# A threshold for one short weight block, the place of two sigmoid gates among weight splits, and the turn of six transposes in a two-layer fp32 kernel

## The chip, the cores and the metric

The kernel runs on one core of one Trainium2 chip. The metric is the device time of one execution in microseconds (us); lower is better.

## The reference

Two transformer layers over 1024 tokens of 1024 channels, batch 1, all in fp32. The first layer is attention of two kinds (eight grouped heads over all tokens, eight heads over a neighbourhood of the 16 x 64 grid). The second has a recurrence (RWKV7) and a latent attention, whose outputs are merged by gates. Cut to what the change touches:

```python
def mla_branch(c_q, c_kv, k_pe, z, positions, g_q, w_uq, g_kv, w_ukv, w_out_b):
    q = (rmsnorm(c_q, g_q) @ w_uq).reshape(bsz, seq, B_HEADS, QK_NOPE_DIM + QK_ROPE_DIM)
    kv = (rmsnorm(c_kv, g_kv) @ w_ukv).reshape(bsz, seq, B_HEADS, QK_NOPE_DIM + V_HEAD_DIM)
    ...

def second_block(...):
    u = rmsnorm(h, g_pre)
    proj = u @ w_in
    feat_a, z_a, c_q, c_kv, k_pe, z_b, gate_logits = split_cols(proj, ...)
    y_a = rwkv7_branch(feat_a, z_a, ...)
    y_b = mla_branch(c_q, c_kv, k_pe, z_b, ...)
    gates = jax.nn.sigmoid(gate_logits + b_gate)
    g_a, g_b = gates[..., :D_MODEL], gates[..., D_MODEL:]
    merged = g_a * y_a + g_b * y_b
    h = h + rmsnorm(merged @ w_o, g_post)
```

`c_q` (256 columns) and `c_kv` (128 columns) are the "compressed columns" below.

## The kernel before

Five programs, one per engine, are written out by hand (`pe_program`, `act_program`, `dve_program`, `pool_program`, `sp_program`); each waits on semaphores that others raise. There is no scheduler: the order on an engine is the order in which its program issues.

**Products.** Every fp32 matrix product is three matmuls of rounded parts: high by high, high by low, low by high. One such step of 128 rows of the inner dimension is called a product here (L992, L993, L994 in the dense part of the second layer; L695 to L697 in the merges).

**Weights.** The weights come as 52 blocks (`wplan`), each of up to 2048 elements per partition. SyncE fetches block n into one staging tile `WST` (`fetch`, L3103), ScalarE rounds it into a high part in pieces of 512 columns (`part`, L1416), GpSimd subtracts to get the low part (L2809). A fetch waits for the splits of the block before it, since there is one staging tile; a split waits for the end of the block that used the same one of two buffers. TensorE waits on entering a block for its last piece. The class `Weights` is run by every engine's program in step and says when the pieces of the next block are issued; `tick` is called with the products done so far in the block:

```python
while self.coming is not None and self.coming[0] <= self.b + (...) and \
      self.ticks[0] >= (20 if self.b in EARLY else 36) + 9 * self.ticks[1]:
    self.ticks[1] += 1
    self.split(False)
    if self.b in EARLY:
        self.fetch_next()
```

So the four pieces of the successor come after 36, 45, 54 and 63 products, and in blocks that are in `EARLY` after 20, 29, 38 and 47, with the next fetch issued as soon as the staging tile is free. `leave` issues what is left at the end of the block. Most blocks count 96. `OUT1` is 13, so `OUT1 + 5` is block 18: the last 160 columns ahead of the paired blocks, which counts 8 tiles x 8 steps x 3 x 160/512 = 60.

**The second layer's input product** (`dense_walk`) goes through blocks 17 to 37. The first ones (17, 18, half of 19) run alone. After that, `Interleave` mixes the dense products with the recurrence: 16 `unit`s in two flows; after every round of unit steps `fill` issues as many dense products as fit beside them. At the end, a third generator, `late`, is advanced once per turn, each turn with a fill of 2.2 us of dense products: it squares the compressed columns (L1806), sums them (L2589), raises the mean to the power -1/2 on GpSimd (L2815), scales the columns (L2603, L2604 on VectorE), transposes them (L1218 on TensorE, six groups of four), and splits them into high and low (L1813 on ScalarE, L2609 on VectorE). Each engine's `late` counts turns, so that the steps stand at the right place of its program. What is left of the dense products comes in `rest`.

**Merges.** Eight blocks of 256 output columns (`MERGES`), four groups of 12 matmuls each. Per 128 columns a gate is loaded by SyncE into one of two tiles `GA` (L3390) and goes through a sigmoid on ScalarE (`output_gate`, L1942); VectorE multiplies (L2753, L2758), adds the branches (L2760), and ScalarE and VectorE split the sum for the output product (L1962, L2735). `ahead`, at a block's start, issues the whole split of the next block. TensorE takes the eight PSUM banks in turn for the groups.

Of the kernel before, what the change touches and what calls it, by code (L numbers as in the profile page):

```python
# [148 lines left out]
def build(nc, a, out):  # L149
    ctx = ExitStack()  # L150
    with ctx:
# [194 lines left out]
        wplan = []  # L346
# [89 lines left out]
        half_p, w_lo, power_p, rope_p, zero_p, prep_p, lat_p, band_lo = by(  # L436
            POOL, "half_p", "w_lo", "power_p", "rope_p", "zero_p", "prep_p", "lat_p", "band_lo")

        EARLY = (0, 1, 2, 3, OUT1 - 1, OUT1, OUT1 + 1, UQ - 2, UQ - 1, *range(UQ + 2 + len(MERGES), len(wplan) - 1))

        class Weights:

# [220 lines left out]
        def pe_program(e, w):  # L663
# [544 lines left out]
                yield NORM_US  # L1208

            def late():  # L1210
                for _ in range(LANDED + 8):
                    yield
                for g in range(2):
                    for k in range(3):
                        ps = bank_at(("ct", k, g), k, (lat_a, ("ct", k, g)), (lat_v, ("ct", k, g)))
                        w.wait_ge(*lat_v["cn", 4 * g + 3])
                        for i in range(4):
                            m = e.transpose(ps[:, tile128(i)], CN[:, 4 * g + i, tile128(k)], ident)  # L1218
                        m.then_inc(lat_tr.sem, lat_tr.up(("ct", k, g)))
                        yield  # L1220
# [179 lines left out]
        def act_program(e, w):  # L1400
# [399 lines left out]
            def late():  # L1800
                for _ in range(LANDED):
                    yield
                for x in range(4):
                    w.wait_ge(*d_cn[x // 2]["all"])
                    two = slice(2 * x, 2 * x + 2)
                    e.activation(SQC[:, two, :], CN[:, two, 0:384], ACT.Square).then_inc(lat_a.sem, lat_a.up(("sq", x)))  # L1806
                    yield
                for _ in range(4):
                    yield
                for g in range(2):  # L1810
                    for k in range(3):
                        w.wait_ge(*lat_tr["ct", k, g])
                        e.activation(CTH[:, k, half512(g)], psum(("ct", k, g)), ACT.Identity, scale=vec("g_q", k) if k < 2 else vec("g_kv")).then_inc(  # L1813
                            lat_a.sem, lat_a.up(("ct", k, g)))
                        yield
# [129 lines left out]
            for x, (br, n) in enumerate(MERGES):  # L1945
                wt.enter()
                wt.ahead()
                for c in range(2):
                    u = 2 * x + c
                    ct = 2 * n + c  # L1950
                    if u == 0:
                        output_gate(0)
                    for j in ((0,), (1, 2, 3))[c] if x == 0 else ():
                        w.wait_ge(*d_ya[j]["in"])
                        e.activation(YAH[:, j, :], YAL[:, j, :].bitcast(F), ACT.Copy).then_inc(merge_a.sem, merge_a.up(("ya", j)))
                    for half in range(2):
                        wt.tick(12)
                        if half and u + 1 < 2 * len(MERGES):
                            output_gate(u + 1)
                        if br == 0:  # L1960
                            w.wait_ge(*merge_v[x, c, half, "sum"])
                            e.activation(AH[:, ct, half512(half)], M2[half][:, :], ACT.Copy).then_inc(merge_a.sem, merge_a.up(("m", ct, half)))  # L1962
# [14 lines left out]
        def dve_program(e, w):  # L1977
# [602 lines left out]
            def late():  # L2580
# [20 lines left out]
                for g in range(2):  # L2601
                    for i in range(4 * g, 4 * g + 4):
                        e.tensor_scalar(CN[:, i, 0:256], CN[:, i, 0:256], STAT[:, 96 + 2 * i:97 + 2 * i], None, ALU.mult).then_inc(*latent(("cq", i)))  # L2603
                        e.tensor_scalar(CN[:, i, 256:384], CN[:, i, 256:384], STAT[:, 97 + 2 * i:98 + 2 * i], None, ALU.mult).then_inc(*latent(("cn", i)))  # L2604
                    yield
                for g in range(2):
                    for k in range(3):
# [875 lines left out]
```

## Time and profile before

| | |
|---|---|
| median of 3 runs | 1895.66 us (1895.03 to 1895.91) |
| the profiled execution | 1894.98 us |
| its span | 1893.2 us |
| TensorE matmul busy | 1828.9 us (97%) |
| VectorE busy | 953.0 us (50%) |
| ScalarE busy | 793.1 us (42%) |
| GpSimd busy | 410.1 us (22%) |
| mean granted TensorE clock | 0.995 of full |

The span is from the first to the last instruction; 1.8 us lie around it. Busy time of TensorE counts matmuls; its weight loads overlap. The idle time of TensorE (some 64 us in all) is spread over many waits; the profile says for each which engine's instruction ended it, or "issue" where it shows no releaser.

### The profile page before, as it was taken

Reading aid. Unit: us, or ns where it says so; the run is one execution under the profiler, and the core shown is the slowest. Engines: PE = TensorE matmul, PEld = TensorE weight load, DVE = VectorE, ACT = ScalarE, POOL = GpSimd, SP = SyncE. Lnnn points to the kernel's source line nnn. Section 1 sums busy time; section 2 is a strip of 40 time slices with the busy share of each in tenths; the row PEclk is TensorE's granted clock in tenths of the full one; section 3 lists DMA queues with packets and bytes.
Section 4 is the critical chain, followed back from the end, with each engine's and each line's share of the span. In section 5 each row is a group of like instructions: output and inputs, shape, how many; then the busy total and the mean of one; then the engine's idle time right before and its main releaser. Section 6 shows DMA issues by size and latency. Waiting matters only on the chain.

```text
span 1893.2 us, 37184 instructions
## 1 busy us (share of the span) xinstructions
PE 1828.9 (97%) x15473; PEld 1478.4 (78%) x15473; DVE 953.0 (50%) x2056; ACT 793.1 (42%) x1725; POOL 410.1 (22%) x416
## 2 busy tenths in 40 slices
PE   6999999999999999999999999999999999999998
PEld 6997766888887789777777778777777786667887
DVE  5677766233344353135554465544653347774523
ACT  5346666343454343223343333333432346654421
POOL 4550000111213421312222222222221301001321
PEclk9999999999999999999999999999999999999999
DMA  5153310334323332330221222212113221005442
GB/s 189 38 170 95 86 40 1 103 99 129 103 87 106 112 134 89 108 106 27 85 60 50 68 67 62 75 50 81 61 42 99 76 64 46 1 1 175 148 156 89
DMA packets 145903, 159.81 MB, mean 84 GB/s; under 512 B 15076, under 2 KB 123944, under 8 KB 145736
## 3 DMA queue, kind: packets, MB, share of 16 engines
q1 hardware_dynamic: 145512, 156.44, 25.9%
q8 instruction: 123, 2.02, 0.4%
q0 software_dynamic: 224, 0.99, 0.1%
q14 instruction: 44, 0.36, 0.1%
HBM read 110.53 MB, written 52.62 MB: 86 GB/s over the span
## 4 chain that ended last, share of the span: by engine, by line
PE 89%; ACT 4%; DVE 3%; POOL 2%; DMA 2%; issue 1%; POOLq 0%; DVEq 0%; SPq 0%; ACTq 0%
PE ps L992 8%; PE ps L994 7%; PE ps L993 7%; PE ps L695 7%; PE ps L697 7%; PE ps L696 7%; PE ps L1103 4%; PE ps L805 3%; PE ps L784 3%; PE ps L884 3%; PE ps L886 3%; PE ps L885 3%; PE ps L792 3%; PE ps L1289 3%; PE ps L1140 3%; PE ps L1312 2%
## 5 line engine op out<-in xcount | busy, mean ns | idle before, releaser
L2809 POOL TENSOR_TENSOR t<-t,t 128x512 fp32r<-128x512 f32 x183 | 240.2, 1325 | 868.2 <-ACT t L1416 855.0
L992 PE MATMUL ps<-t,t 128*128 128x512 f32 (+2 forms) x720 | 293.0, 407 | 3.6 <-issue 2.3
L695 PE MATMUL ps<-t,t 128*128 128x256 f32 (+2 forms) x872 | 283.0, 325 | 3.1 <-issue 1.6
L696 PE MATMUL ps<-t,t 128*128 128x256 f32 (+2 forms) x872 | 277.1, 318 | 0.0
L697 PE MATMUL ps<-t,t 128*128 128x256 f32 (+2 forms) x872 | 277.1, 318 | 0.0
L994 PE MATMUL ps<-t,t 128*128 128x512 f32 (+2 forms) x720 | 269.6, 374 | 0.0
L993 PE MATMUL ps<-t,t 128*128 128x512 f32 (+2 forms) x720 | 269.4, 374 | 0.0
L695 PEld LDWEIGHTS ps<-t,t 128*128 128x128 f32 x872 | 166.5, 191 | 19.7 <-issue 8.4
L696 PEld LDWEIGHTS ps<-t,t 128*128 128x128 f32 x872 | 166.7, 191 | 10.3 <-issue 0.4
L697 PEld LDWEIGHTS ps<-t,t 128*128 128x128 f32 x872 | 166.4, 191 | 10.4
L992 PEld LDWEIGHTS ps<-t,t 128*128 128x128 f32 x720 | 137.0, 190 | 32.5 <-issue 9.9
L994 PEld LDWEIGHTS ps<-t,t 128*128 128x128 f32 x720 | 136.7, 190 | 25.7
L993 PEld LDWEIGHTS ps<-t,t 128*128 128x128 f32 x720 | 137.3, 191 | 15.9
L2120 DVE TENSOR_REDUCE t<-ps 128x1 f32<-128x1024 f32 (+7 forms) x128 | 126.4, 988 | 35.6 <-PE ps L784 34.2
L2815 POOL TENSOR_TENSOR t<-t,t 128x1 f32<-128x1 f32 (+3 forms) x68 | 66.8, 982 | 337.8 <-DVE t L2405 138.6
L1416 ACT ACTIVATE t<-t 128x512 fp32r<-128x512 f32 x182 | 107.4, 622 | 58.7 <-DMA t<-in_w_out 30.9
L1691 ACT ACTIVATE t<-ps 128x512 f32<-128x512 f32 (+2 forms) x90 | 49.5, 550 | 147.0 <-PE ps L994 146.8
L884 PE MATMUL ps<-t,t 128*128 128x512 f32 x256 | 101.1, 395 | 0.0
L885 PE MATMUL ps<-t,t 128*128 128x512 f32 x256 | 99.9, 390 | 0.0
L886 PE MATMUL ps<-t,t 128*128 128x512 f32 x256 | 99.9, 390 | 0.0
L1103 PEld LDWEIGHTS ps<-t,t 64*64 64x64 f32 x2304 | 72.2, 135 | 19.3 <-issue 14.0
L1103 PE MATMUL ps<-t,t 64*64 64x64 f32 x2304 | 80.9, 221 | 1.3 <-DVE t L2483 1.0
(277 smaller groups left out, 3272.6 us busy)
## 6 DMA issues: line engine op xcount, KB each, us to landing
t<-in_w_in SPq DMA_DIRECT2D x53, 512.0 KB, 5.9
zgate_spill<-t SPq DMA_DIRECT2D x20, 512.0 KB, 3.1
tile_bias<-t SPq DMA_DIRECT2D x16, 576.0 KB
t<-tile_bias SPq DMA_DIRECT2D x8, 1152.0 KB, 6.3
t<-zgate_spill SPq DMA_DIRECT2D x16, 512.0 KB, 4.3
feat_spill<-t SPq DMA_DIRECT2D x13, 512.0 KB, 3.2
tile_bias<-band_bias SPq DMA_DIRECT2D x48, 128.0 KB
t<-values_and_gates SPq DMA_DIRECT2D x96, 64.0 KB
```

Of the source, the lines that this page charges most:

```text
L695: e.matmul(dst, lh, rh, start=k == 0, stop=False)
L696: e.matmul(dst, lh, rl, start=False, stop=False)
L697: m = e.matmul(dst, ll, rh, start=False, stop=k == n - 1)
L884: e.matmul(dst, AH[:, x, tile128(i)], hi[:, k, :], start=x == 0, stop=False)
L885: e.matmul(dst, AH[:, x, tile128(i)], lo[:, k, :], start=False, stop=False)
L886: m = e.matmul(dst, AL[:, x, tile128(i)], hi[:, k, :], start=False, stop=x == 7)
L992: e.matmul(dst, lh, rh, start=k == 0, stop=False)
L993: e.matmul(dst, lh, rl, start=False, stop=False)
L994: m = e.matmul(dst, ll, rh, start=False, stop=k == 7)
L1103: i = e.matmul(ps[pq, 64 * x:64 * x + 64], lhs(pq, x), rhs(pq, x), start=True, stop=True)
L2120: e.tensor_reduce(NMX[:, z % 16:z % 16 + 1], src, X, ALU.max, negate=True).then_inc(top.sem, top.up(key or z))
L2809: e.tensor_tensor(WLO[wslot(b)][:, o], WST[:, o], WHI[wslot(b)][:, o].bitcast(F), ALU.subtract).then_inc(w_lo.sem, w_lo.up((b, p)))
```

## The change

Three edits.

1. Block 18 is put into `EARLY`: its successor's four pieces come at counts 20, 29, 38 and 47 rather than 36, 45, 54 and at `leave`; and block 20 is fetched inside block 18.
2. The `late` generators of TensorE, ScalarE and VectorE wait two turns longer before the transposes, the high parts and the low parts. VectorE's two turns come one behind each half of the scaling.
3. In the merges, the gate of a block's first 128 columns is issued by ScalarE behind `ahead` of the same block, where it was issued ahead of the last split of the sum in the block before.

```diff
-        EARLY = (0, 1, 2, 3, OUT1 - 1, OUT1, OUT1 + 1, UQ - 2, UQ - 1, *range(UQ + 2 + len(MERGES), len(wplan) - 1))
+        EARLY = (0, 1, 2, 3, OUT1 - 1, OUT1, OUT1 + 1, OUT1 + 5, UQ - 2, UQ - 1, *range(UQ + 2 + len(MERGES), len(wplan) - 1))
...
# pe_program, late
-                for _ in range(LANDED + 8):
+                for _ in range(LANDED + 10):
...
# act_program, late
-                for _ in range(4):
+                for _ in range(6):
...
# act_program, merges
-                    if u == 0:
-                        output_gate(0)
+                    if c == 0:
+                        output_gate(u)
...
-                        if half and u + 1 < 2 * len(MERGES):
+                        if half and c == 0:
                             output_gate(u + 1)
...
# dve_program, late (inside the loop over the two halves)
                     yield
+                    yield
```

What this moves, first on ScalarE in block 18 (L1416 is a piece of block 19's split, L1691 copies a finished tile out of PSUM, L1679 is the sine of the angles). Before:

```order
L1691 ACTIVATE t_139<-ps 128x160 x2
L1679 ACT_TABLE_LOAD
L1679 ACTIVATE t_241<-t_241 128x128
L1679 ACTIVATE t_242<-t_242 128x128
L1691 ACTIVATE t_139<-ps 128x160 x2
L1416 ACTIVATE t_52<-t_51 128x512
L1691 ACTIVATE t_140<-ps 128x160
L1416 ACTIVATE t_52<-t_51 128x512
L1691 ACTIVATE t_140<-ps 128x160 x2
L1416 ACTIVATE t_52<-t_51 128x512
L1691 ACTIVATE t_140<-ps 128x160
L1416 ACTIVATE t_52<-t_51 128x512
```

Now, behind the same first row:

```order
L1416 ACTIVATE t_52<-t_51 128x512
L1679 ACT_TABLE_LOAD
L1679 ACTIVATE t_241<-t_241 128x128
L1679 ACTIVATE t_242<-t_242 128x128
L1691 ACTIVATE t_139<-ps 128x160
L1416 ACTIVATE t_52<-t_51 128x512
L1691 ACTIVATE t_139<-ps 128x160
L1691 ACTIVATE t_140<-ps 128x160
L1416 ACTIVATE t_52<-t_51 128x512
L1691 ACTIVATE t_140<-ps 128x160
L1416 ACTIVATE t_52<-t_51 128x512
L1691 ACTIVATE t_140<-ps 128x160 x2
```

The fourth piece stood behind the eighth and last tile's copy; it now stands behind the sixth's, with two copies after it. On SyncE, block 20's fetch now stands ahead of the second store of this block's columns instead of behind it.

In the late part, on ScalarE (L1813 is a high part of the compressed columns, L1416 into t_52 a piece of block 37). Before:

```order
L1813 ACTIVATE t_228<-ps,t_57 128x512
L1691 ACTIVATE t_141<-ps 128x512
L1813 ACTIVATE t_228<-ps,t_57 128x512 x3
L1691 ACTIVATE t_141<-ps 128x512
L1813 ACTIVATE t_228<-ps,t_57 128x512 x2
L1416 ACTIVATE t_52<-t_51 128x512
L1691 ACTIVATE t_139<-ps 128x512
L1416 ACTIVATE t_52<-t_51 128x512
```

Now:

```order
L1691 ACTIVATE t_141<-ps 128x512
L1813 ACTIVATE t_228<-ps,t_57 128x512 x2
L1691 ACTIVATE t_141<-ps 128x512
L1813 ACTIVATE t_228<-ps,t_57 128x512 x2
L1416 ACTIVATE t_52<-t_51 128x512
L1813 ACTIVATE t_228<-ps,t_57 128x512
L1691 ACTIVATE t_139<-ps 128x512
L1813 ACTIVATE t_228<-ps,t_57 128x512
L1416 ACTIVATE t_52<-t_51 128x512
```

On TensorE, 10 products stood between the last recurrence sum (L1032) and the first group of transposes (L1218), and 15 stand there now; the last two groups are now two products apart from the fourth, with a piece of block 37's split ahead of the fifth's high part. Before, two of the six groups stood behind the first products of block 36 (or at its border); now four do.

In the merges, on ScalarE, a piece of the difference (L1942 is a gate, L1955 rounds the recurrence's output, L1416 a piece of the next block's split, L1962 the high part of a sum):

```order
 L1942 ACTIVATE t_257<-t_257,t_57 128x1024
 L1955 ACTIVATE t_254<-t_255 128x1024 x3
+L1416 ACTIVATE t_52<-t_51 128x512 x2
 L1942 ACTIVATE t_256<-t_256,t_57 128x1024
-L1416 ACTIVATE t_52<-t_51 128x512 x2
 L1942 ACTIVATE t_257<-t_257,t_57 128x1024
+L1416 ACTIVATE t_53<-t_51 128x512 x2
 L1942 ACTIVATE t_256<-t_256,t_57 128x1024
-L1416 ACTIVATE t_53<-t_51 128x512 x2
 L1962 ACTIVATE t_49<-t_259 128x512
 L1942 ACTIVATE t_257<-t_257,t_57 128x1024
 L1962 ACTIVATE t_49<-t_260 128x512
```

The split of two pieces has passed the gate (into t_256) that stood ahead of it; the same happens at each of the seven later blocks.

## Rows read from the trace of the kernel before

**Rows 1.** The page: span, TensorE's line, the granted clock in 40 slices.
```profile
span 1893.2 us, 37184 instructions
PE 1828.9 (97%) x15473; PEld 1478.4 (78%) x15473; DVE 953.0 (50%) x2056; ACT 793.1 (42%) x1725; POOL 410.1 (22%) x416
PEclk9999999999999999999999999999999999999999
```

**Rows 2.** TensorE's waits, whole span: line, releaser: us in total, times, longest.
```profile
PE ps L1032 <- POOL t L2961: 9.5, 7, 3.4
PE ps L1218 <- DVE t L2604: 4.0, 1, 4.0
...
PE ps L992 <- issue: 2.3, 1, 2.3
...
PE ps L695 <- issue: 1.6, 1, 1.6
```

**Rows 3.** Windows: us, busy of PE, PEld, DVE, ACT, POOL, PEclk, DMA, GB/s.
```profile
765.10:768.40 3.30, 3.30 (x9) 2.56 (x9) 0.00 (x0) 0.00 (x0) 0.00 (x0) 0.50 0.98 259
768.50:771.80 3.30, 3.30 (x16) 2.72 (x16) 0.00 (x0) 0.31 (x1) 0.00 (x0) 1.00 0.21 50
1482.30:1485.10 2.80, 2.77 (x9) 2.41 (x10) 2.47 (x9) 0.69 (x1) 0.00 (x0) 0.50 0.04 9
...
1735.00:1738.30 3.30, 3.30 (x15) 2.73 (x16) 0.06 (x1) 0.00 (x0) 0.00 (x0) 1.00 0.66 221
...
829.90:833.20 3.30, 3.30 (x11) 2.63 (x10) 2.61 (x6) 0.42 (x1) 2.21 (x3) 0.50 0.00 0
```

**Rows 4.** Timeline of ScalarE in block 18: start, us, line, tiles [idle before].
```profile
745.83 0.30 ACT L1691 ACTIVATE t<-ps 128x160 f32<-128x160 f32 x1 [2.38 <-PE ps L994]
...
756.55 0.30 ACT L1691 ACTIVATE t<-ps 128x160 f32<-128x160 f32 x1 [1.86 <-PE ps L994]
...
762.11 0.62 ACT L1416 ACTIVATE t<-t 128x512 fp32r<-128x512 f32 x1
```

**Rows 5.** Timeline of GpSimd and SyncE, and TensorE's entry into block 19.
```profile
762.81 1.26 POOL L2809 TENSOR_TENSOR t<-t,t 128x512 fp32r<-128x512 f32 x1 [1.39 <-ACT t L1416]
...
741.37 1.66 SPq L3103 DMA_DIRECT2D t<-in_w_in  x2
...
764.17 0.47 PE L992 MATMUL ps<-t,t 128*128 128x512 f32 x1 [2.30 <-issue]
```

**Rows 6.** Line 3103's fetches from 741 to 765 us: time to landing.
```profile
DMA to landing us min/median/max: 4.0/5.2/6.2
```

**Rows 7.** Timeline of TensorE at the first transposes.
```profile
1476.82 0.39 PE L992 MATMUL ps<-t,t 128*128 128x512 f32 x1
...
1477.50 0.39 PE L992 MATMUL ps<-t,t 128*128 128x512 f32 x1
...
1482.33 1.08 PE L1218 MATMUL ps<-t,t 128*128 128x128 f32 x4 [3.99 <-DVE t L2604]
```

**Rows 8.** Timeline of VectorE and GpSimd there.
```profile
1478.51 1.28 DVE L2604 TENSOR_SCALAR t<-t,t 128x128 f32<-128x128 f32 x1
...
1481.91 0.27 DVE L2604 TENSOR_SCALAR t<-t,t 128x128 f32<-128x128 f32 x1
...
1477.15 3.77 POOL L2809 TENSOR_TENSOR t<-t,t 128x512 fp32r<-128x512 f32 x3
```

**Rows 9.** Timeline of ScalarE in the first two merges, and of the output product.
```profile
1724.15 3.16 ACT L1955 ACTIVATE t<-t 128x1024 fp32r<-128x1024 f32 x3
1730.40 1.15 ACT L1942 ACTIVATE t<-t,t 128x1024 f32<-128x1024 f32 x1 [3.10 <-DMA t<-zgate_spill]
1731.46 1.14 ACT L1416 ACTIVATE t<-t 128x512 fp32r<-128x512 f32 x2
...
1825.01 0.60 ACT L1972 ACTIVATE t<-ps 128x512 f32<-128x512 f32 x1 [18.03 <-PE ps L886]
```

**Rows 10.** Timeline of GpSimd and VectorE in the merges.
```profile
1732.33 2.52 POOL L2809 TENSOR_TENSOR t<-t,t 128x512 fp32r<-128x512 f32 x2 [18.55 <-ACT t L1416]
...
1728.01 2.35 DVE L2745 TENSOR_TENSOR t<-t,t 128x1024 fp32r<-128x1024 f32 x2
...
1741.08 0.69 DVE L2758 TENSOR_TENSOR t<-ps,t 128x512 f32<-128x512 f32 x1 [6.02 <-ACT t L1942]
...
1802.43 1.47 DVE L2735 TENSOR_TENSOR t<-t,t 128x512 fp32r<-128x512 f32 x2
```

**Rows 11.** SyncE's fetch of block 42 and TensorE's entry into it.
```profile
1719.78 0.65 SPq L3103 DMA_DIRECT2D t<-in_w_out_a  x1
...
1734.95 0.47 PE L695 MATMUL ps<-t,t 128*128 128x512 f32 x1 [1.63 <-issue]
```

## The prediction

> **What bounds the kernel now.** I read the page first: of a span of 1893.2 us TensorE's matmuls are busy for 1828.9, and the granted clock rounds to full in every slice [rows 1]. So only TensorE's idle time, some 64 us, and stretches at the lower clock can be given back, and an edit on another engine counts only where TensorE waits for it. The second view is the list of TensorE's waits [rows 2]. Three of its lines lie at the places of the three edits: 4.0 us at L1218 for VectorE's L2604 (the first transposes), 2.3 us at L992 and 1.6 us at L695, both shown as "issue". The largest line of the second layer, 9.5 us at L1032 for GpSimd, is in the recurrence, which the change leaves alone. Third, the timelines around the three stalls, to see what TensorE really waits for and what the engines did before. Fourth, the windows behind each stall [rows 3]: behind the 2.3 us and behind the 4.0 us the granted clock is 0.50 (1.2 GHz) for some 3 us and then 1.00 (2.4 GHz) again; behind the 1.6 us it stays at 1.00.
>
> **Edit 1, block 18.** Block 19's fourth piece is issued by ScalarE at 762.11, behind the last tile's copy [rows 4], GpSimd's subtraction follows from 762.81 for 1.26, and TensorE's first product of block 19 starts at 764.17 after 2.30 us of idleness [rows 5]. It is the wait for this piece; the trace puts it under "issue" only because the releaser's record doesn't match. Now the piece stands behind the sixth tile's copy, which ends at 756.85 [rows 4]: 756.9 + 0.6 for ScalarE and 1.3 for GpSimd gives 758.8, 3 us before TensorE comes (764.17 - 2.30 = 761.87). The first piece now comes behind the second tile's copy (746.1) [rows 4] and may wait there for its weights: the fetch is issued at 741.37 to 743.03 [rows 5] and lands 4.0 to 6.2 us later [rows 6], so by 749.2 at the latest. That holds back ScalarE by up to 3 us, with a copy of a tile and the sine behind it; TensorE has eight banks and takes 2.68 us per tile (the distance of the copies [rows 4]: 756.55 - 745.83 over four tiles), so it doesn't notice. The fetch of block 20 moves ahead of a store on SyncE's queue, and waits there for the fourth piece, done at 758.8, when the store's own data is ready only after 762: nothing is held back. Gain: **2.30**.
>
> Then the clock. From 765.10 to 768.40 TensorE gets 9 matmuls done at 0.50, in the next equal stretch 16 at 1.00 [rows 3]: 7 x 0.23 = **1.6**. With the stall gone I take the fall to be gone, since it comes 1 us behind the stall and is the only one within 60 us. Bounds: 0 (the fall has another cause or was by chance) to 1.6. The Trainium skill (TensorE: Matmul & The Clock Gate, Part 1: The HAM clock gate) says that what the gate judges by isn't aligned to the kernel's start, so that the same idle time may cost the lower clock in one execution and not in another. By that rule this term is 1.6 in some executions of the kernel before and 0 in others, and the sum against the median would be up to 1.6 smaller; one profile can't show it.
>
> **Edit 2, the transposes.** TensorE's last product before the transposes starts at 1477.50 (products are 1477.50 - 1476.82 = 0.68 apart), and the first group starts at 1482.33, after 3.99 us [rows 7]. It waits for the fourth scaled tile, VectorE's L2604 from 1481.91 for 0.27 [rows 8]. The edit puts five more products ahead of the first group: 5 x 0.68 = **3.4** of the 3.99 are filled, 0.6 stay. The work is only moved: `rest` is five products shorter, whose place is before the next phase, on TensorE too. What hides the 3.4 is VectorE's chain, so if that chain ends later, the rest of the wait grows one for one. It is made slow by its neighbour: L2604 takes 1.28 us while GpSimd's three subtractions run, 0.27 afterwards [rows 8]. Their order is unchanged, so I take the same. The clock: between 1482.30 and 1485.10 TensorE runs at 0.50, 2.8 us [rows 3] that at full rate are worth 1.4. The 0.6 that stay are shorter than the 1.6 us behind which the clock stayed at 1.00 [rows 2, 3], so I take **1.4** as gone; bounds 0 and 1.4. What comes behind the two moved turns: ScalarE's fifth high part now stands behind a piece of block 37, which may wait for its weights. Nobody but VectorE's low part waits for it there, the keys need it only 30 us later, and the bank that it reads isn't reused. The border to block 36 is reached some 5 us sooner, and its pieces are all done at 1480.9 [rows 8], before the transposes even start. Blocks 37 to 39 are fetched from that border on, so their chain moves with TensorE.
>
> **Edit 3, the merges.** ScalarE is free at 1727.3, and sits until 1730.40 for a gate's data; only then come gate and split (1731.46), GpSimd's two subtractions (1732.33 to 1734.85), and TensorE's block 42 at 1734.95, 1.63 late [rows 9, 10, 11]. With the split first, it starts when its weights and its buffer are there: the fetch is issued at 1719.78 [rows 11], and lands at the latest 6.2 later [rows 6], 1726.0. So ScalarE splits at 1727.3 to 1728.5, GpSimd is done about 1730.5, TensorE wants it at 1733.3. Gain: **1.6**, no clock term. The gate isn't later: its data lands at 1730.4 whatever ScalarE does. In the later merges the gates do get later, since the split ahead of them waits for TensorE to leave the buffer (and in three of them a high part of a sum waits for VectorE first). A merge's gate then comes 2.3 us (1.14 + 1.15 [rows 9]) to some 4 us (an estimate: two more operations of VectorE of 0.69 [rows 10] ahead) behind the block's start, where VectorE wants it after 12 x 0.23 = 2.7. VectorE's lag grows by up to 1.3. TensorE feels that only by its banks, eight groups or 21.8 us behind; in the trace VectorE's worst lag is about 3.4 (1741.08 [rows 10] against the end of the group at 1734.95 + 2.7). At the end of the merges VectorE is done at 1803.9 [rows 10]; what it makes last is read behind the first half of the output product, whose second half gives its first result at 1825.0 [rows 9], 2.7 after it began. Some 18 us of cover: cost 0.
>
> **Sum.** 2.30 + 1.6 + 3.4 + 1.4 + 1.6 = 10.3 us off the profiled execution's own 1894.98 gives 1884.7. The median of the runs, 1895.66, is 0.7 above that execution. The likeliest median is thus between 1884.7 and 1885.4; I take **1885.0**.
>
> **Rivals.**
>
> *A, the clock gives nothing back* (0.16). The falls move to other stalls. For it: a fall also stands behind GpSimd's wait in the recurrence (829.90, [rows 3]), where the edits change nothing, and seven such waits are there [rows 2]; shifted by some microseconds, another of them may catch one. Against: falls stand only behind the longest. Gain 2.3 + 3.4 + 1.6 = 7.3, time 1887.7 to 1888.4.
>
> *B, one of the three stalls stays or moves* (0.12). The weakest are the transposes, since they have no slack at all, and block 42. If VectorE's chain ran 2 us later against TensorE, edit 2 would leave 2.6 us and, being longer than the 2.3, its clock fall: 2.0 + 1.4 lost, time 1888.4. For block 42: VectorE's two L2745 run from 1728.01 for 2.35 [rows 10], just when GpSimd now subtracts. At most the two take turns, 1728.0 + 2.35 + 2.52 = 1732.9 [rows 10], 0.4 before TensorE comes, so the gain holds by a little; if not, up to 1.6 is lost. (The Trainium skill, SBUF, Who interferes with whom, has such a rule: VectorE and GpSimd share one pair of ports under an exclusive lock. L2604's 1.28 against 0.27 agrees.)
>
> *C, the edits do nothing that can be measured* (0.07). The waits are inferred, and the two under "issue" have no named releaser; if both had another cause and the transposes' wait returned, the time would be within 0.2% (3.8 us, about what a measurement of this kernel can tell from no change): 1892 to 1899. Against: the times of pieces and entries fit to 0.1 us.
>
> *D, slower* (0.04). The late gates reach TensorE. Place: the banks of the merges. If VectorE's lag at a gate didn't dissolve within a merge, it would add up, and from a lag of eight groups (21.8 us) on, TensorE would pay split and gate, 2.3 us, at each of six borders, and a lower clock behind two of them: 1885.0 + 13.8 + 3.2 = 1902. Against: a lag of 3.4 now, and four groups of VectorE's work fit into a merge.
>
> **How the numbers follow.** The forecast as summed has 0.61, A 0.16, B 0.12, C 0.07, D 0.04. The forecast's own range is 1882.8 (the fall at 829.90 absent too, 1.6, and the 0.6 filled) to 1886.5; A and B reach to 1888.4 and, with both partly, to 1890. The range is 1882.5 to 1890.0, with C and D outside. Faster by over 0.2%: forecast, A and B, 0.89, less 0.01 for mixtures; within 0.2%: 0.08; slower: 0.04.
>
> **What would show it.** Right: no 2.3 at L992 and no 1.6 at L695 among TensorE's waits; L1218's wait below 1 us; the granted clock at 1.00 behind blocks 18's and the transposes' places; TensorE's busy time down by about 3 us and its idle time by 7; GpSimd done with block 42 before TensorE comes. Wrong in edit 2: VectorE's fourth L2604 further behind the start of GpSimd's three subtractions than the 4.8 us here [rows 8]. Wrong in edit 3: a wait for VectorE at a merge's matmul. Wrong in the clock terms: a window at 0.50 behind a wait that is here at 1.00.

## The result, and the profile after

The changed kernel takes **1884.68 us** (median of 4 runs, 1883.75 to 1885.09) where the kernel before takes 1895.68 (median of 4 runs beside it, 1895.03 to 1895.91): ratio 0.9941, 95% interval 0.9929 to 0.9953. That is 11.0 us faster; forecast were 10.7 (1885.0). The profiled execution took 1885.09, with a span of 1883.2; the prediction's sum, made from the profiled execution of before, was 1884.7.

Below, the lines of the page of after (span, busy times, the granted clock in 40 slices), which answer to [rows 1]:

```profile
span 1883.2 us, 37184 instructions
PE 1826.0 (97%) x15473; PEld 1476.3 (78%) x15473; DVE 950.3 (50%) x2056; ACT 792.4 (42%) x1725; POOL 408.6 (22%) x416
PEclk9999999999999999999999999999999999999999
```

The number of instructions is the same. TensorE's busy time is 2.9 us lower (1828.9 to 1826.0); its idle time, span less busy time, went from 64.3 to 57.2, by 7.1. So 10.0 us of span went, split nearly as the prediction had them: 7.3 of waits (2.30, 3.4, 1.6) and 3.0 of clock (1.6, 1.4). TensorE's waits of after, the lines that answer to [rows 2] (line, releaser: us in total, times, longest; below L2605 every line of the code has moved down by one):

```profile
PE ps L1032 <- POOL t L2962: 9.5, 7, 3.4
...
PE ps L1218 <- DVE t L2604: 0.6, 1, 0.6
PE ps L695 <- issue: 0.3, 1, 0.3
```

The 2.3 at L992 is not there any more, 4.0 has become 0.6, 1.6 has become 0.3, and the recurrence's 9.5 is untouched. The windows of after (us, busy of PE, PEld, DVE, ACT, POOL, PEclk, DMA, GB/s), at about the same times as two of [rows 3] and at the recurrence's:

```profile
765.00:768.40 3.40, 3.40 (x17) 2.82 (x16) 0.00 (x0) 1.01 (x2) 0.00 (x0) 1.00 0.00 0
826.60:830.00 3.40, 3.40 (x9) 2.64 (x8) 3.19 (x7) 0.23 (x1) 1.62 (x2) 0.50 0.00 0
1481.80:1485.20 3.40, 3.40 (x18) 2.80 (x18) 1.13 (x2) 1.76 (x3) 0.00 (x0) 1.00 0.26 93
```

Behind block 18 and behind the transposes the clock is now full (17 and 18 matmuls in 3.4 us where 10 and 9 were); the fall behind GpSimd's wait in the recurrence has moved forward with everything else, from 829.9 to 826.6, and is still there.

**Block 18.** Timelines of after: ScalarE's first and last piece, GpSimd's last, and TensorE's entry into block 19.

```profile
748.05 0.63 ACT L1416 ACTIVATE t<-t 128x512 fp32r<-128x512 f32 x1 [1.95 <-DMA t<-in_w_in]
...
756.71 0.62 ACT L1416 ACTIVATE t<-t 128x512 fp32r<-128x512 f32 x1
...
757.41 1.29 POOL L2810 TENSOR_TENSOR t<-t,t 128x512 fp32r<-128x512 f32 x1 [1.39 <-ACT t L1416]
...
761.67 0.43 PE L992 MATMUL ps<-t,t 128*128 128x512 f32 x1
```

The first piece waited 1.95 us for its weights, as foreseen, and nobody noticed. The fourth is done by GpSimd at 758.7 (forecast 758.8), 3.0 us before TensorE enters block 19 without a wait.

**The transposes.** VectorE's scalings and GpSimd's three subtractions, and TensorE:

```profile
1473.22 1.37 DVE L2603 TENSOR_SCALAR t<-t,t 128x256 f32<-128x256 f32 x1 [1.40 <-POOL t L2816]
1474.51 1.31 DVE L2604 TENSOR_SCALAR t<-t,t 128x128 f32<-128x128 f32 x1
1475.75 1.40 DVE L2603 TENSOR_SCALAR t<-t,t 128x256 f32<-128x256 f32 x1
...
1477.98 0.27 DVE L2604 TENSOR_SCALAR t<-t,t 128x128 f32<-128x128 f32 x1
...
1473.15 3.84 POOL L2810 TENSOR_TENSOR t<-t,t 128x512 fp32r<-128x512 f32 x3
...
1478.40 0.63 PE L1218 MATMUL ps<-t,t 128*128 128x128 f32 x4 [0.62 <-DVE t L2604]
```

The fourth L2604 starts 4.83 us behind the start of GpSimd's three, against 4.76 in [rows 8]: the chain is as slow as before, and TensorE now works beside it.

**The first merge border.** ScalarE, SyncE's fetch, GpSimd, VectorE, and TensorE's entry into block 42, which answer to [rows 9 to 11]:

```profile
1716.24 2.94 ACT L1955 ACTIVATE t<-t 128x1024 fp32r<-128x1024 f32 x3
1720.99 1.16 ACT L1416 ACTIVATE t<-t 128x512 fp32r<-128x512 f32 x2 [1.80 <-DMA t<-in_w_out_a]
1722.27 1.15 ACT L1942 ACTIVATE t<-t,t 128x1024 f32<-128x1024 f32 x1
...
1710.88 0.39 SPq L3104 DMA_DIRECT2D t<-in_w_out_a  x1
...
1721.88 2.98 POOL L2810 TENSOR_TENSOR t<-t,t 128x512 fp32r<-128x512 f32 x2 [16.75 <-ACT t L1416]
...
1720.11 2.35 DVE L2746 TENSOR_TENSOR t<-t,t 128x1024 fp32r<-128x1024 f32 x2
...
1724.96 0.47 PE L695 MATMUL ps<-t,t 128*128 128x512 f32 x1 [0.29 <-issue]
```

The split is ahead of the gate, but it doesn't start as ScalarE comes free (1719.2). It waits 1.80 us for its weights, which land some 10 us behind their issue. GpSimd is done at 1724.86, and TensorE waits 0.29. Of this landing the prediction said at most 6.2.

### The profile page after: what moved, and what is told of

It reads as the page before. It is cut to its first block, busy times and chain, and to the rows that moved or that the text cites. A ratio compares the mean times of both kernels' runs of the same rounds, so it can differ in the third digit from the quotient of the medians.

```text
span 1883.2 us, 37184 instructions
## 1 busy us (share of the span) xinstructions
PE 1826.0 (97%) x15473; PEld 1476.3 (78%) x15473; DVE 950.3 (50%) x2056; ACT 792.4 (42%) x1725; POOL 408.6 (22%) x416
## 4 chain that ended last, share of the span: by engine, by line
PE 89%; ACT 4%; DVE 3%; DMA 2%; POOL 2%; issue 1%; POOLq 0%; DVEq 0%; SPq 0%; ACTq 0%
PE ps L992 8%; PE ps L994 7%; PE ps L993 7%; PE ps L695 7%; PE ps L697 7%; PE ps L696 7%; PE ps L1103 4%; PE ps L805 3%; PE ps L784 3%; PE ps L884 3%; PE ps L886 3%; PE ps L885 3%; PE ps L792 3%; PE ps L1289 3%; PE ps L1140 3%; PE ps L1312 2%
## 5 line engine op out<-in xcount | busy, mean ns | idle before, releaser
L992 PE MATMUL ps<-t,t 128*128 128x512 f32 (+2 forms) x720 | 291.7, 405 | 1.5 <-POOL t L2810 1.5
L695 PE MATMUL ps<-t,t 128*128 128x256 f32 (+2 forms) x872 | 283.0, 325 | 1.8 <-DVE t L1998 1.3
L695 PEld LDWEIGHTS ps<-t,t 128*128 128x128 f32 x872 | 166.6, 191 | 18.4 <-issue 7.0
L992 PEld LDWEIGHTS ps<-t,t 128*128 128x128 f32 x720 | 136.3, 189 | 30.0 <-issue 7.7
L1416 ACT ACTIVATE t<-t 128x512 fp32r<-128x512 f32 x182 | 107.4, 622 | 77.2 <-DMA t<-in_w_out 31.5
L1691 ACT ACTIVATE t<-ps 128x512 f32<-128x512 f32 (+2 forms) x90 | 49.5, 550 | 142.8 <-PE ps L994 142.5
```

What stands on the lines that cost most here:

```text
L695: e.matmul(dst, lh, rh, start=k == 0, stop=False)
L992: e.matmul(dst, lh, rh, start=k == 0, stop=False)
```

## The experiments

Twelve runs in three groups, each group on a chip of its own, with its own runs of the kernel before beside it (medians 1895.74, 1897.09 and 1896.23). The change itself was run again in the second group alone, so the runs of the third (first border alone, and all under "A better version?") are compared with it by their ratios. A gain is the ratio's: 1896 times what it lies below 1, so 0.001 is 1.9 us. "Half clock" is the time that TensorE's granted clock was at 0.50 in the profiled execution, without its first 20 and its last 2 us.

### One edit at a time

**Block 18 alone.**

```diff
-        EARLY = (0, 1, 2, 3, OUT1 - 1, OUT1, OUT1 + 1, UQ - 2, UQ - 1, *range(UQ + 2 + len(MERGES), len(wplan) - 1))
+        EARLY = (0, 1, 2, 3, OUT1 - 1, OUT1, OUT1 + 1, OUT1 + 5, UQ - 2, UQ - 1, *range(UQ + 2 + len(MERGES), len(wplan) - 1))
```

> Edit 1 alone (block 18 in EARLY, nothing else changed). Theory 'wait and clock' (each edit removes its own wait of TensorE, and the fall of the clock behind a long wait goes with it): 2.3 + 1.6 = 3.9 us less than before, about 1891.8; no wait at L992 in block 19, the granted clock at 1.00 from 757 to 775 us, the 4.0 us at L1218 and the 1.6 us at L695 unchanged. Theory 'wait alone' (the falls of the clock are not caused by the waits): 2.3 us less, about 1893.4, and a stretch at 0.50 still near 765. Theory 'one edit carries all' (the gain of the whole change came from another edit): 1895.7.

Measured: 1891.62 us (1889.51 to 1893.96), ratio 0.9977 [0.9967, 0.9988]: 4.4 us faster (4.1 by the medians). TensorE's waits have no "issue" at L992 any more; 4.0 at L1218 stay. The term of edit 1 is 2.30 + 1.6 = 3.9: it holds. One thing was expected otherwise: the wait ahead of block 42 is 1.9 here and not 1.6.

**The transposes two turns later alone.**

```diff
-                for _ in range(LANDED + 8):
+                for _ in range(LANDED + 10):
...
-                for _ in range(4):
+                for _ in range(6):
...
+                    yield
```

> Edit 2 alone (transposes two turns later). 'Wait and clock': 3.4 + 1.4 = 4.8 us less than before, about 1890.9; L1218's wait 0.6, no stretch at 0.50 behind it; the 2.3 us at block 19 with its stretch at 0.50 still there. 'Wait alone': 3.4 us less, about 1892.3, a stretch at 0.50 still near 1480. 'One edit carries all': either 1885 or 1895.7.

Measured: 1891.33 us (1889.72 to 1892.89), ratio 0.9976 [0.9968, 0.9985]: 4.6 us faster (4.4 by the medians). The wait at L1218 is 0.6, and the clock behind it is full. The term was 3.4 + 1.4 = 4.8.

**The gates behind the splits alone.**

```diff
-                    if u == 0:
-                        output_gate(0)
+                    if c == 0:
+                        output_gate(u)
...
-                        if half and u + 1 < 2 * len(MERGES):
+                        if half and c == 0:
```

> Edit 3 alone (gates behind the splits). Both theories of the clock say the same here, since the clock stayed at 1.00 behind this wait: 1.3 us less than before, about 1894.4, with 0.3 us left at L695, as in the whole change. Rival 'the late gates cost something later': less than 1.3, with a wait for VectorE at a merge's or the output product's matmuls.

Measured: 1893.36 us (1892.78 to 1894.81), ratio 0.9989 [0.9981, 0.9998]: 2.1 us faster (2.4 by the medians). No wait of L695 under "issue" is left at all, where 0.3 was expected to stay. The three gains add up to 10.9 by the medians (11.0 by the ratios), against 11.0 of the whole: **the edits add up**, and no fourth gain is to be seen, though each gain alone is uncertain by some 2 us. The gain of this one was expected to be 1.3, as in the profile of after, and lies above that and above the 1.6 that the prediction gave edit 3; the interval (0.4 to 3.6 us) holds all of them.

**The kernel before once more**, unchanged, for a second profile of it.

> The kernel before, unchanged, profiled once more, for the clock. If a fall follows from the length of the wait alone, the stretches at 0.50 stand where they stood: behind the attention's end (about 601 us), at 765, 830 and 1482. If where the wait falls against the gate's own rhythm matters, one or more of them is missing or a new one has come, the one behind the shortest wait (2.3 us, at 765) first; the time then differs by 1.6 per fall.

Measured: 1896.98 us, span 1895.1. Its waits are 4.0, 2.3 and 2.1 at the three places (1.6 in the other profile), and the falls of the clock aren't the same. Windows of this second profile (columns as above):

```profile
765.00:768.40 3.40, 3.40 (x17) 2.79 (x16) 0.00 (x0) 0.00 (x0) 0.00 (x0) 1.00 0.76 214
...
1479.80:1486.60 6.80, 5.79 (x18) 4.85 (x19) 3.98 (x14) 1.97 (x3) 0.00 (x0) 0.50 0.01 4
1735.80:1739.20 3.40, 3.40 (x9) 2.63 (x8) 0.00 (x0) 0.00 (x0) 0.00 (x0) 0.50 0.81 296
```

Behind the same 2.3 us nothing falls this time; behind the 4.0 us the clock is low for 6.8 us and not for 3.4, and behind block 42, where the prediction had "no clock term", it is low for 3.4. The two profiles of before thus show 1.6 + 1.4 + 0 and 0 + 2.9 + 1.7 at the three places (the latter are half of the matmuls' time in these windows). Over all the profiled executions:

| the stall | us | clock at 0.50 behind it |
|---|---|---|
| block 19's entry | 2.3 | 5 of 7 (before, transposes alone, one turn, GpSimd's wait, first border alone) |
| the transposes | 4.0 | 5 of 5, four times for 6.8 us and once for 3.4 |
| the transposes, one turn later | 2.6 | 0 of 1 |
| block 42's entry | 1.9 to 2.1 | 3 of 3 |
| block 42's entry | 1.5 to 1.7 | 0 of 3 |
| the transposes, filled by two turns or by GpSimd's wait | 0.6 to 0.9 | 0 of 5 |

Two of the rows on block 42's entry, in block 18 alone (low behind it, from 1733.2) and in GpSimd's wait (below; not low):

```profile
1732.35 0.47 PE L695 MATMUL ps<-t,t 128*128 128x512 f32 x1 [1.90 <-issue]
```

```profile
1731.22 0.47 PE L695 MATMUL ps<-t,t 128*128 128x512 f32 x1 [1.73 <-issue]
```

So which falls a profile shows is in part chance. This agrees with what the Trainium skill says (TensorE: Matmul & The Clock Gate, Part 1: The HAM clock gate), that what the gate judges by isn't aligned to the kernel's start: the same 2.3 us cost the clock in 5 executions of 7.

The sum over the kernel isn't steady either. Half clock is 17.0 us in both profiles of before, but 20.5 with block 18 alone (a stall fewer), 20.5 with the transposes alone, 13.7 with the gates alone, and 10.2 with one turn, where all three places still have a stall; 10.2 is also what both profiles of the change have. Every execution has its mean granted clock on record, and in the 57 of before beside these runs the time goes with it: 1897.8 us on average at 0.993 (14 executions), 1894.8 at 0.996 (16).

**The gate behind the split at the first border alone**, to see whether the 2.4 is that border's.

```diff
-                    if u == 0:
-                        output_gate(0)
+                    if u in (0, 2):
+                        output_gate(u)
...
-                        if half and u + 1 < 2 * len(MERGES):
+                        if half and u != 1 and u + 1 < 2 * len(MERGES):
```

> The kernel before, with a gate put behind its split at the first border between merge units alone (unit 1 to unit 2); the last two units keep the gate ahead of the split. Theory A (all of edit 3 is the one TensorE wait ahead of block 42's first product): the wait of 1.6 to 2.1 there goes and the whole of the 2.4 that edit 3 alone gave is here too, some 1893.3 against 1895.7, 2.1 to 2.6 us faster. Rival B (the later borders give something as well, or cost something): less than 1.3 us faster, or over 3.3.

Measured: 1893.8 us (1891.84 to 1895.47), ratio 0.9986 [0.9977, 0.9995]: 2.7 us faster (2.4 by the medians). Theory A holds: all of edit 3 is the one wait ahead of block 42. The later gates give nothing and cost nothing that can be measured. 2.4 fits 1.6 to 2.1 of wait, and 1.7 more in those executions in which the clock falls behind it; how often it does is known from six profiles only.

### How far the transposes have to go, and why

**One turn later** (the kernel before with one turn).

```diff
-                for _ in range(LANDED + 8):
+                for _ in range(LANDED + 9):
...
-                for _ in range(4):
+                for _ in range(5):
...
+                yield
```

> The kernel before, with the transposes ONE turn later. Two products stand ahead of the first group that didn't before: L1218's wait goes from 4.0 to about 2.6 us. 'Wait and clock' with the gate's own rhythm: 1.4 us from the wait, and of the clock's 1.4 to 3.4 behind it a part, since 2.6 us of idleness is caught in some executions only: 1.4 to 3 us less than before on the same chip. 'Wait alone': 1.4 less. A step of 4.8 at once would mean that it isn't the products in front that fill the wait.

Measured: 1895.05 us (1891.5 to 1897.73), ratio 0.9987 [0.9979, 0.9996]: 2.5 us faster (2.0 by the medians). TensorE:

```profile
1482.62 0.63 PE L1218 MATMUL ps<-t,t 128*128 128x128 f32 x4 [2.64 <-DVE t L2604]
```

2.64 are left of 3.99: 1.35 are filled, two products of 0.68. Two turns fill 3.37 (3.99 - 0.62), that is five products of 0.68. The first turn is worth two products and the second three: what is filled goes with the products, not with the turns.

**Three turns later** (the change with one turn more).

```diff
-        LANDED, LATE_STEPS = 8, 10
+        LANDED, LATE_STEPS = 8, 11
...
-                for _ in range(LANDED + 10):
+                for _ in range(LANDED + 11):
...
-                for _ in range(6):
+                for _ in range(7):
...
+                yield
```

> The changed kernel with the transposes one turn later still (three instead of two), and one more turn at the end for them. Three more products stand in front, 2.0 us, of which 0.6 are wanted: L1218's wait goes from 0.6 to 0, 0.6 us less than the changed kernel, if nothing behind waits for the transposes. Rival: they are now late for what follows, and a wait at the keys (L695) or at the bank of a dense product appears; then equal or slower.

Measured: 1884.54 us (1884.04 to 1884.83), ratio 0.9935 [0.9924, 0.9947]; the change beside it (below) 1884.14. TensorE's waits have no L1218 any more: the 0.6 are filled, and the span of the profiled execution is 1882.2 against 1882.6. In the medians nothing of the 0.6 can be seen. Two turns are enough.

**GpSimd waits for the first four scalings** (the kernel before with one line more). The stall is VectorE's, and the question is what makes VectorE late.

```diff
                 power(STAT[:, 96:112], STAT[:, 80:96], 16, "latent")
+                w.wait_ge(*lat_v["cn", 3])
```

> The kernel before, with one wait more: GpSimd, behind its power, waits for the fourth scaled tile before it goes on with the three subtractions of block 36. Theory 'neighbour' (VectorE's L2603 and L2604 are slow because GpSimd works at the same time): L2603 0.34 and L2604 0.27 from the first on, the fourth tile 3.1 us sooner, L1218's wait 4.0 - 3.1 = 0.9 us, and 3.1 plus the clock behind it (1.4 to 3) less in time, 1891 to 1892.6, without moving any transpose. Rival 'they are slow by themselves' (first use of the tiles): no change of the wait, 1895.7.

Measured: 1890.92 us (1890.33 to 1891.36), ratio 0.997 [0.9958, 0.9982]: 5.7 us faster (6.2 by the medians), and no product has been moved. VectorE, GpSimd and TensorE there:

```profile
1477.82 0.35 DVE L2603 TENSOR_SCALAR t<-t,t 128x256 f32<-128x256 f32 x1 [1.40 <-POOL t L2815]
1478.09 0.28 DVE L2604 TENSOR_SCALAR t<-t,t 128x128 f32<-128x128 f32 x1
...
1479.92 1.39 DVE L2604 TENSOR_SCALAR t<-t,t 128x128 f32<-128x128 f32 x1
1481.24 0.34 DVE L2603 TENSOR_SCALAR t<-t,t 128x256 f32<-128x256 f32 x1
1481.50 1.38 DVE L2604 TENSOR_SCALAR t<-t,t 128x128 f32<-128x128 f32 x1
...
1479.82 4.54 POOL L2809 TENSOR_TENSOR t<-t,t 128x512 fp32r<-128x512 f32 x3 [2.04 <-DVE t L2604]
...
1479.89 0.63 PE L1218 MATMUL ps<-t,t 128*128 128x128 f32 x4 [0.91 <-DVE t L2604]
```

With GpSimd held back, the first four pairs of scalings take 0.34 to 0.35 and 0.28 each, and TensorE waits 0.91. Once GpSimd starts, three scalings take 1.38 to 1.39: **each of its three subtractions costs VectorE one scaling that is 1.0 to 1.1 longer**, wherever the three are put. In the kernel before, those three stand ahead of the transposes: (1.37 - 0.35) + (1.28 - 0.28) + (1.37 - 0.34) = 3.05, and 0.91 + 3.05 = 3.96, the 3.99 of the stall. So 3.05 us of the stall that edit 2 fills come from two engines working side by side. The Trainium skill (SBUF — State Buffer, Who interferes with whom) has the rule: VectorE in its faster mode and GpSimd share a pair of ports under an exclusive lock, and one blocks for the other's whole instruction. The rows agree, one long scaling for one subtraction; that there are ports behind it, and in which mode VectorE runs, no row shows.

**The change once more**, unchanged, beside the others of this call.

> The changed kernel, once more on this chip, as what e6 is compared with, and for its clock: 11 us less than before. By 'wait and clock', with no wait over 0.6 left at the three places, no stretch at 0.50 near 765, 1480 or 1730 in this execution either, while those behind the attention (about 600) and in the recurrence (about 828) may come and go.

Measured: 1884.14 us (median of 6 runs, 1883.35 to 1885.24 in five of them and 1894.93 in one), ratio 0.9943 [0.9926, 0.9961]; half clock 10.2 us as in the first profile of the change. As expected, nothing is at 0.50 near 765, 1480 or 1730. At block 42's entry no wait is listed this time (0.3 in the first profile). The one run at 1894.93 has no profile; its mean granted clock is 0.947 where the five others have 0.997 or 0.998, and why stays open.

### A better version?

**GpSimd's wait in place of edit 2**: edits 1 and 3, and the wait.

```diff
+        EARLY = (0, 1, 2, 3, OUT1 - 1, OUT1, OUT1 + 1, OUT1 + 5, UQ - 2, UQ - 1, *range(UQ + 2 + len(MERGES), len(wplan) - 1))
...
+                    if c == 0:
+                        output_gate(u)
...
+                        if half and c == 0:
...
+                w.wait_ge(*lat_v["cn", 3])
```

> Edits 1 and 3 of the change, and in place of edit 2 (the transposes two turns later) a wait on GpSimd: it starts its three sums of 128x512 behind VectorE's scalings of the compressed columns and not beside them. Theory (the 4.0 at the transposes is VectorE slowed down by GpSimd: its scalings took 1.3 to 1.4 us each beside GpSimd's sum, 0.27 to 0.34 without): the scalings take 0.27 to 0.35 each, the wait at the transposes is 0.9 as in the run with this wait alone, and the time is that of the change and 0.3: 1884.9, within 0.5. Rival (the wait delays GpSimd's sums, 2.7 us later, and with them a product behind them): 1886 or more, with a new wait of TensorE on GpSimd.

Measured: 1884.39 us (1883.72 to 1885.6), ratio 0.9937 [0.9923, 0.995]. Within the noise, one line on GpSimd is worth as much as edit 2's two turns. TensorE waits 0.94 at the transposes and nowhere new: GpSimd's subtractions now start 2.0 us behind the first scaling (1474.58 against 1472.57) where they started with it, and nobody needs them so early.

**Three turns, and the last gain's transfer behind block 42's weights.** The 0.3 at L695 of the change was still to be had. The three turns are as above; the rest of the edit is this:

```diff
-            e.dma_start(GP[:, :], a["g_post_2"].partition_broadcast(128)).then_inc(d_gp.sem, d_gp.up("all"))
...
+                if x == 1:
+                    e.dma_start(GP[:, :], a["g_post_2"].partition_broadcast(128)).then_inc(d_gp.sem, d_gp.up("all"))
```

> The change with three turns more for the transposes in place of two, and with the transfer of the last gain issued in the loop of the merges, behind block 42's weights, in place of before it. With the splits first, ScalarE waits 1.8 us for block 42's weights (landed some 10 us after their issue) and TensorE is left a wait of 0.3 ahead of its first product. Theory (the gain's transfer takes the weights' room in the queues): the weights land 0.5 to 2 us sooner and the 0.3 is gone, 1884.2 against 1884.5 of three turns alone. Rival (the weights wait for earlier and larger transfers): nothing moves, 1884.5, and the 0.3 of three turns alone, if it has it, is still there.

Measured: 1883.77 us (1883.28 to 1885.02), ratio 0.9934 [0.9921, 0.9946], no different from three turns alone (0.9935). But the rows say more than the time. ScalarE, VectorE, GpSimd and TensorE at the first border:

```profile
1719.47 1.16 ACT L1416 ACTIVATE t<-t 128x512 fp32r<-128x512 f32 x2 [0.18 <-DMA t<-in_w_out_a]
...
1720.21 3.45 DVE L2747 TENSOR_TENSOR t<-t,t 128x1024 fp32r<-128x1024 f32 x2
...
1720.36 4.44 POOL L2811 TENSOR_TENSOR t<-t,t 128x512 fp32r<-128x512 f32 x2 [15.35 <-ACT t L1416]
...
1724.91 0.47 PE L695 MATMUL ps<-t,t 128*128 128x512 f32 x1 [0.36 <-issue]
```

The weights do land sooner: ScalarE has them 8.6 us behind the fetch's issue at 1710.91, against 10.1 in the change's first profile, 9.5 in its second and 9.4 with three turns alone (one turn has 8.6 too, with the transfer ahead, so that the transfer is the cause is not shown). But the 0.3 isn't gone, as the theory had it. With three turns alone GpSimd's pair is done 13.6 us behind the fetch's issue (issued 1710.20), here 13.9, although it starts 0.9 sooner behind it (9.45 for 10.32), and TensorE waits 0.36 where three turns alone has no such wait:

```profile
1720.52 3.29 POOL L2811 TENSOR_TENSOR t<-t,t 128x512 fp32r<-128x512 f32 x2 [15.88 <-ACT t L1416]
```

GpSimd's two subtractions now run beside all of VectorE's two L2747. They take 4.44 where 2.52 [rows 10] is their time beside no other engine's work but VectorE's L2753, which reads PSUM and is itself no longer for it (1.29 for two, as alone); VectorE's two take 3.45 for 2.35. In the change they meet in part only (2.98). What the earlier landing gave, the neighbour took, and a little more.

The starts and ends of the two pairs tell what limits GpSimd at this border. In all seven profiles in which they meet, GpSimd is done 4.6 to 4.8 us behind the start of VectorE's pair, whether it starts 0.15 us behind it (here) or 1.8 (the change: 1720.11 to 1724.86). That is the turn-taking of the prediction's rival B, which allowed 2.35 + 2.52 = 4.87. TensorE comes 4.56 us behind the start of VectorE's pair in the change, 5.31 in the profile of before that the prediction was read from, and 4.6 to 4.9 in the five other profiles with a wait there. So where the pairs meet, an earlier landing wins no more than some 0.2 us. The meeting costs TensorE 0 to 0.4 us, and not the 1.6 that rival B had at most.

**All of it and GpSimd's wait.**

```diff
+                w.wait_ge(*lat_v["cn", 3])
```

> The run with three turns and the later gain, and GpSimd's wait as well. Theory (the wait at the transposes is paid once, by the turns or by the wait): nothing is left there to gain, and the time is that of three turns and the later gain within 0.5 us, 1884.2. Rival (the slow-down of VectorE still costs TensorE through something behind it): 1 us faster or more, 1883.2 or less.

Measured: 1884.13 us (1882.89 to 1884.58), ratio 0.9933 [0.9921, 0.9946]. The wait and the turns pay for the same stall once. With the gain's transfer later again, the weights land 7.9 us behind their issue, GpSimd's pair takes 4.44 again and is done 0.1 before TensorE starts block 42, with no wait listed there. No version of these is measurably faster than the change: the ratios are 0.9933 to 0.9937 for its 0.9941, with intervals that overlap.

## Why the prediction was right

**What bounds the kernel**: right. The whole gain is TensorE's idle time (7.1) and its slow stretches (2.9), and every other engine's busy time is within 3 us of what it was.

**Edit 1**: right in both terms for the profiled execution (2.30 of wait gone, 765.1 back at full clock), and 3.9 against 4.1 to 4.4 measured alone (interval 2.3 to 6.3 us). The steps hold too: the fourth piece done at 758.7 for 758.8, a wait of 1.95 for the first, hidden by the banks. The bound of 0 on the clock term is real as well: the second profile of before has no fall there, nor has the gates' run.

**Edit 2**: the fill is right to 0.1 (five products, 3.37; 0.62 stay). The chain is as slow as before, as assumed, and the run with GpSimd's wait shows why. **The clock term was mis-sized**: 1.4 stands for a fall of 2.8 to 3.4 us, and four of the five profiled executions with this stall show 6.8 us, worth 2.9. Its upper bound of 1.4 was too low.

**Edit 3**: the sign and the mechanism are right, and three numbers off. First, "lands at the latest 6.2 later" was the wrong row: 6.2 is the longest landing of block 18's fetches, and this fetch of block 42, read by itself, has in the kernel before

```profile
DMA to landing us min/median/max: 9.2/9.2/9.2
```

That was hidden, because in the kernel before the split stood behind a gate that came later still (1730.40 against a landing at 1729.0). ScalarE then starts the split not at "1727.3 to 1728.5" but at 1729.0; with 0.9 until GpSimd follows and its 2.52 that makes 1732.4, still 0.9 ahead of TensorE (1733.3). Second, in the change the landing takes 10.1, and beside VectorE's last pair GpSimd takes 2.98, so that 0.29 of the 1.63 stayed: 1.3 and not 1.6 in this execution, while the second profile of the change lists no wait there. VectorE's pair, and not the landing, is what would have held GpSimd next. Third, "no clock term" was right for that execution and the two others with 1.5 to 1.7; in three more the wait was 1.9 to 2.1, and the clock fell behind each. With the wait gone in full (1.5 to 2.1) and 1.7 of clock in half of the executions, 2.4 for edit 3 is accounted for; that this is its make-up is argued from six profiles, not shown. The cover of the late gates held: VectorE's last low part is done at 1794.1, the output product's second half gives its first result at 1815.04.

```profile
1792.62 1.47 DVE L2736 TENSOR_TENSOR t<-t,t 128x512 fp32r<-128x512 f32 x2
...
1815.04 0.60 ACT L1972 ACTIVATE t<-ps 128x512 f32<-128x512 f32 x1 [18.71 <-PE ps L886]
```

**The sum** came out right to 0.4 us for the profiled execution, and that is in part luck. Its clock terms were read from one execution of before, with 1.6 + 1.4 + 0 at the three places, where the second one has 0 + 2.9 + 1.7. That is 3.0 us in one and 4.6 in the other. Over the whole kernel both have 17.0 us of half clock, but that is no rule: the profiles with one edit, or with one turn, have 10.2 to 20.5. The transposes' clock was put too low, block 42's at nothing, and block 18's at its full 1.6, which 5 of 7 executions show.

**Rivals.** A (the clock gives nothing back) fell: none of the profiles of the change shows a fall at a new place. The reason given against it, "falls stand only behind the longest", was wrong, though. The same trace has a fall of 6.8 us behind the end of the attention, where TensorE had three waits of 0.5 to 0.9 us within 4 us and was busy for 1.99 of the last 3.40; it is in every profile, for 3.4 or 6.8 us:

```profile
601.20:608.00 6.80, 6.35 (x34) 4.38 (x31) 6.56 (x14) 4.88 (x14) 4.73 (x4) 0.50 0.05 17
```

B fell for the transposes and came in part, 0.3 us, for block 42. C is excluded by the interval. D fell: putting the later gates ahead again (first border alone) changes nothing that can be measured, and no wait of TensorE for VectorE came up in the merges.

## What to carry to other kernels

Look at what the engine beside the late one does at the same moment: VectorE's chain was 3.05 us late by GpSimd's three subtractions alone, and one wait on GpSimd was worth as much as a new order of TensorE's work. When a wait in front of an operation goes, the next one behind it was hidden and has to be read by its own row, not by its like elsewhere (9.2 us of landing for 6.2). A slow clock behind a wait should be priced over several executions, and not from one profile, neither stall by stall nor over the whole kernel (10.2 to 20.5 us of half clock in kernels that differ by one stall).

## What the runs showed of the hardware

- The granted clock fell behind 1.9 to 2.1 us at block 42's entry (3 of 3) and not behind 1.5 to 1.7 (0 of 3) or the 2.6 of one turn (0 of 1); behind 2.3 us it fell in 5 executions of 7. At the end of the attention it fell in all 14, behind two to four short waits of which none was over 0.9 us. It was low for 3.4 or for 6.8 us each time, never for anything between, and twice as long behind the same 4.0 us in four executions of five.
- An fp32 scaling of VectorE (128x128 or 128x256, 0.27 to 0.35 us) took 1.28 to 1.40 beside a 128x512 subtraction of GpSimd, one scaling for each subtraction; the three subtractions themselves took 3.77 to 4.54. VectorE's two 128x1024 subtractions and GpSimd's two of 128x512 went from 2.35 and 2.52 to 3.45 and 4.44 where they ran side by side from the start (2 profiles). Where GpSimd came in 0.6 to 0.9 us before VectorE's pair ended, VectorE's kept its 2.35 and GpSimd's took 2.98 to 3.29 (5 profiles).
- The same fetch of 128x1024 weights had landed 8.6 to 10.1 us behind its issue in the twelve profiles with a broadcast transfer of a gain right ahead of it on SyncE, and 8.5 and 7.9 in the two with that transfer behind it. With a spread of 1.5 us in the twelve, two are too few to say how much of it is that transfer.
